# The slab behind a rewriting norm: its high part cut in quarters inside ScalarE's loop, its low part in halves between two evacuations, and TensorE begun by halves

## The chip, the cores and the metric

The kernel runs on one core of a Trainium2 chip. The metric is the device time of one launch in microseconds (us). Shown is the median of three runs; the profile is a fourth execution.

## The reference, cut to what matters

The model is a stack of four transformer-like layers on 512 tokens of width 1024: two of one kind and two of a second kind. In the second kind a layer begins with a norm that is modulated by a condition:

```python
shift1, scale1, gate1, shift2, scale2, gate2 = jnp.split(mod[:, None, :], 6, axis=-1)
h = rms_norm_2(x, norm1) * (1.0 + scale1) + shift1
proj = h @ w_in
```

The product `h @ w_in` has 1816 columns: a pooling part `u`, queries `q`, keys and values `kv` of three branches, and 24 gates. They feed a pooling mixer and sparse attention. After them come an output projection, a second norm and a feed-forward part. The change concerns only the first projections of these two layers, so it acts at two places of the run. They are called place 1 (layer 0 of the second kind, about 2015 to 2110 us of the profile) and place 2 (layer 1, about 2615 to 2710 us).

## The kernel before

**Slabs.** All weights pass through two slab buffers of 128 x 2048 words. SyncE loads slab i into `raw[i % 2]` with two DMAs of 512 KB (L323), once the low part of slab i-2 is made. ScalarE rounds it to `w_hi` (L329) and VectorE subtracts to get `w_lo` (L333). TensorE then forms `w_hi*h_hi + w_hi*h_lo + w_lo*h_hi` in three matmuls for each 128 x 128 block (`THREE`). A slab of a projection has 256 output columns: eight row blocks k of 256 words each, so words 0 to 1023 hold k = 0 to 3. It fills two PSUM banks, "piece" 0 and 1. One call of `proj_piece_T` makes 24 matmuls (L384) for one piece.

**The rewriting norm.** Call the slabs at such a norm S, S+1, S+2 and so on. TensorE multiplies slab S by `x` times the gain alone, before the norm's factor `rstd` is known; the norm's sums and its broadcast are formed between these matmuls. Once `rstd` is known the activations are rewritten with their factor and shift, for the slabs that follow. Per row block i, VectorE makes `nbuf` (L2460), ScalarE makes `h_hi` (L1942) and VectorE makes `h_lo` (L2467); TensorE's chunk i of slab S+1 (six matmuls, L459) waits for `h_lo` i. VectorE's step i+1 of L2460 comes before its step i of L2467. After its eight steps ScalarE goes on to `beside_projection`.

**What follows the loop.** For slab S the helper `beside_projection` has ScalarE make `w_hi` of slab S+2 (L329). VectorE takes the two banks of slab S out with the factor `rstd` (L1510, each adding 1 to the semaphore `scaled`). It then waits for both, adds to `evac_dve`, and makes `w_lo` of slab S+2 (L333). ScalarE adds a bias to the two results (L1520). TensorE starts slab S+2 once `w_lo_done`, `evac_act` and `evac_dve` are there.

**What waits for `scaled` besides.** SyncE's queue is one sequence: two loads of compression weights of 1 MB each with a small one behind each (L1317, L1319), then the load of slab S+2, then

```python
sp.wait_ge(s["scaled"], 2 * (ph[1] + 1))
sp.dma_start(pool_w, ...)                      # L1322
```

and only behind it the load of slab S+3. `pool_w` lies in the buffer `rstd`, which both evacuations read.

**From slab S+3 back to TensorE.** For slab S+1 ScalarE makes `w_hi` of slab S+3 first (it waits for the load), and then copies one bank out (L1525). VectorE waits for that copy, builds the compression windows (four operations at L2847) and then makes `w_lo` of slab S+3 (L333, a "late" split). TensorE, done with slab S+2, forms head sums (16 small matmuls, L959) and then begins slab S+3 in a helper that fills in between the compression matmuls (L604, L1858). Its first matmul needs `w_lo` of slab S+3.

Every place where a part of a slab is split is written out by hand; nothing plans it.

Of the kernel before, what the change touches and what calls it, by code (L numbers as in the profile page):

```python
# [58 lines left out]
class Cursor:  # L59


    def __init__(self):
        self.slab = 0
        self.proj = 0
        self.outp = 0
        self.outs = 0
        self.norm = 0
        self.sq = 0
        self.chain = 0
        self.roots = 0  # L70
        self.bcasts = 0
        self.hnorms = 0
        self.order = range(KC)
        self.fresh = False
        self.pending_split = None
        self.late_split = None
        self.pending = None
        self.swiglus = 0
        self.deferred = False
        self.rope = 0  # L80
        self.moved = 0
        self.hn = 0
        self.hnsq = 0
        self.hnb = 0
        self.ret = 0
        self.retg = 0
        self.att = 0
        self.attg = 0
        self.yt = 0
        self.sb = 0  # L90
        self.sbh = 0
        self.pool = 0
        self.base = 0
        self.mid = None
        self.soon = None
        self.third = None
        self.oq = 0
        self.begun = 0
        self.gates = 0
        self.mod = None  # L100
        self.rstds = 0
        self.added = 0
        self.kinds = 1
        self.rewrite = False
        self.first_scaled = False
        self.scaled = 0
        self.rewrites = 0
        self.final = None
        self.mods = 0
        self.just_out = False  # L110
        self.ffs = 0

# [15 lines left out]
def hybrid_stack_kernel(nc, A, out, stop=None):  # L128
# [87 lines left out]
    with ExitStack() as ctx:  # L216
# [78 lines left out]
        s = {}  # L295
        for name in [
            "in_loaded", "first_loaded", "first_hi", "first_lo", "zeroed", "consts_loaded", "bank_done", "bcast_done", "gate_normed", "norm_chain", "x_final", "w_hi_done",
            "w_lo_done", "slab_used", "evac_act", "evac_dve", "a_hi_done", "a_lo_done", "up_normed", "x_ready",
            "sq_done", "sq_added", "sums_done", "sums_copied", "ssq_done", "rms_done", "rstd_done", "h_full", "u_used", "gm_joined", "scaled", "pool_loaded", "h_hi_done", "h_lo_done", "rope_cos",
            "rope_rot", "rope_moved", "rope_sin", "rope_done", "hn_sq", "hn_sum", "hn_ms", "hn_rms", "hn_chain", "hn_bcast",  # L300
            "hn_done", "dv_half", "dv_first", "ff_scaled", "bias_col", "dec_loaded", "ret_s", "ret_p", "ret_o", "ret_copy", "ret_mean", "ret_cen", "ret_gate",
            "ret_y", "att_s", "att_max", "att_exp", "att_t", "att_pt", "att_o", "att_rec", "att_r", "att_rc", "att_w",
            "att_y", "sb_z", "sb_abs", "sb_e", "sb_ln", "sb_sp", "sb_msk", "sb_high", "sb_low", "sb_sum",
            "sb_cut", "sb_a", "sb_exp", "sb_o", "sb_y", "pl_sum", "pl_tail", "pl_x", "pl_mm", "gate_t",
            "gate_sig", "cm_w", "cm_kp", "cm_h", "cm_act", "cm_o", "cm_k", "kd_copy", "cb_s", "cb_sm",
            "cb_sub", "cb_exp", "cb_t", "cb_pt", "cb_mix", "cb_o", "cb_w", "cb_y", "nh_mm", "nh_t", "nh_v", "oq_hi", "oq_lo", "oq_mm", "oq_x", "om_hi", "om_lo", "om_mm", "om_x", "y6_hi", "y6_lo", "mod_silu", "mod_mul", "mod_add", "mod_red",
            "mod_row", "mod_col", "mod_bias", "gmod_one", "gmod_done", "stored", "dve_chain", "act_chain",
            "v_bd",
        ]:
            s[name] = sem(name)  # L310
# [35 lines left out]
        def part_lo(eng, i, part, parts):  # L346

            if part == 0:
                eng.wait_ge(s["w_hi_done"], i + 1)
            cols = slice(part * SLAB // parts, (part + 1) * SLAB // parts)  # L350
            ins = eng.tensor_tensor(w_lo[:, i % 2, cols], raw[:, i % 2, cols], w_hi[:, i % 2, cols].bitcast(F32), ALU.subtract)
            if part == parts - 1:
                ins.then_inc(s["w_lo_done"], 1)

        def step_range(c, n, last):

# [19 lines left out]

        THREE = ((0, 0), (0, 1), (1, 0))

        def proj_piece_T(pe, e, bank, piece, inc, soon=None):
            wbuf, hbuf = (w_hi, w_lo), (h_hi, h_lo)  # L380
            for k in range(KC):
                for n, (a, b) in enumerate(THREE):
                    at = k * 256 + piece * P
                    mm = pe.matmul(ps[:, bank], wbuf[a][:, e % 2, at:at + P], hbuf[b][:, k],  # L384
                                   start=(k == 0 and n == 0), stop=(k == KC - 1 and n == 2))
                if k == 2 and soon:
                    soon()
            if inc:
                mm.then_inc(s["slab_used"], 1)
# [55 lines left out]
        def pe_first_proj(pe, c):  # L445
# [70 lines left out]
            c.rewrite = False  # L516
            c.slab += 1
            c.proj += 1
            return 2

        def pe_proj(pe, c, n, kind):
# [10 lines left out]
            c.just_out = False  # L532
            s0, q0 = c.slab, c.proj

            def step(j, e):
                pe.wait_ge(s["w_lo_done"], j + (s0 + 1))
                if not isinstance(j, int) or q0 + j >= 2:
                    pe.wait_ge(s["evac_act"], j + (q0 - 1))
                    pe.wait_ge(s["evac_dve"], j + (q0 - 1))
                bank = 4 + 2 * ((q0 + e) % 2)  # L540
# [945 lines left out]
        def beside_projection(eng, c, ph, last, split, mine, name, next_ph=None, only=None):  # L1486
            for i in range(len(ph[2])) if only is None else [only]:
                eng.wait_ge(s["slab_used"], c.slab + 1)
                bank = 4 + 2 * (c.proj % 2)
                then_split = False  # L1490
                if split is None:
                    pass
                elif i < len(ph[2]) - 1 or next_ph not in LATE[mine]:
                    then_split = mine == 1 and (c.first_scaled or i == len(ph[2]) - 1 and next_ph == "stick")
                    if not then_split:
                        split(eng, c.slab + 2, c.slab)
                else:

                    c.late_split = lambda n=c.slab: split(eng, n + 2, n)
# [6 lines left out]
                elif c.first_scaled and mine == 1:  # L1506
                    eng.wait_ge(s["rstd_done"], c.rstds)
                    for piece in range(2):
                        dst, src = evac_projection(ph, i, bank, piece)
                        eng.tensor_tensor(dst, src, rstd[:, :], ALU.mult).then_inc(s["scaled"], 1)  # L1510
                    c.scaled += 2
                    eng.wait_ge(s["scaled"], c.scaled)
                    eng.sem_inc(s[name], 1)
                elif c.first_scaled:
                    l = c.rewrites - 1
                    eng.wait_ge(s["bias_col"], 16)
                    for piece in range(2):
                        dst, _ = evac_projection(ph, i, bank, piece)
                        eng.wait_ge(s["scaled"], c.scaled + piece + 1)
                        ins = eng.activation(dst, dst, ACT.Identity, bias=n_bias[:, 2 * l + piece:2 * l + piece + 1])  # L1520
# [5 lines left out]
                elif ph[0] in ("projT", "retention") and mine == 1:  # L1526

                    eng.wait_ge(s["rstd_done"], c.rstds)
                    for piece in range(2):
                        dst, src = evac_projection(ph, i, bank, piece)  # L1530
                        scale = ph[4] if ph[0] == "projT" and ph[4] is not None and i < 2 else 1.0
                        ins = eng.scalar_tensor_tensor(dst, src, scale, rstd[:, :], ALU.mult, ALU.mult)
# [353 lines left out]
        def _(eng):  # L1886
            act_e = nc.scalar
            c = Cursor()
# [5 lines left out]
            for pi, ph in enumerate(phases):  # L1894
                last = pi == last_slabs
                if ph[0] == "norm":
# [35 lines left out]
                    if not c.deferred:  # L1932
                        c.hnorms += 1
                        c.first_scaled = True
                        for i, k in enumerate(c.order):
# [3 lines left out]
                            else:  # L1939
                                eng.wait_ge(s["slab_used"], c.slab + 1)  # L1940
                            at = ph[2][0] * 48 + ph[2][1] * KC + k
                            eng.activation(h_hi[:, k], nbuf[:, i % 2], ACT.Identity, bias=mods[:, at:at + 1]  # L1942
                                           ).then_inc(s["h_hi_done"], 1)
                        c.mods += KC
                        c.rewrites += 1
                    c.bcasts += 1 if ph[3] is None else 2
# [1060 lines left out]
```

## Time and profile before

| what | us |
|---|---|
| median of three runs | 3227.76 |
| lowest, highest | 3224.59, 3228.41 |
| the profiled execution's own time | 3233.87 |
| its span, first to last instruction | 3232.1 |
| TensorE busy | 3201.2 (99%) |
| VectorE busy | 1689.2 (52%) |
| ScalarE busy | 1141.9 (35%) |
| mean granted TensorE clock | 0.996 |

In a timeline row the first number is the start in us from the span's start, the second the time taken. Then come engine, line, operation and operands. A bracket at the end gives how long the engine sat idle before it and what ended that. Matmuls overlap: a row of 0.39 us is followed by the next after 0.23 us, so starts are what to compare.

### The profile page before, as it was taken

The numbers are of one execution on the slowest core, as the hardware profiler recorded it, in microseconds if no ns is written. First come the engines' busy times: TensorE is split into PE (matmuls) and PEld (weight loads), VectorE is DVE, ScalarE is ACT, GpSimd is POOL, SyncE is SP. The second block draws the span as 40 slices with busy tenths as digits, with TensorE's granted clock in tenths as the row PEclk, the third lists the DMA queues.
The fourth block names the chain that finished last, engine by engine and source line by source line (L and its number), as shares of the span: only waits on it lengthen the run. The fifth ranks groups of instructions, "written<-read, shape, count | busy, mean of one in ns | idle before, by whom it ended". The sixth has DMA issues, their size and how long they took to land.

```text
span 3232.1 us, 40590 instructions
## 1 busy us (share of the span) xinstructions
PE 3201.2 (99%) x15504; PEld 2525.9 (78%) x15504; DVE 1689.2 (52%) x2139; ACT 1141.9 (35%) x1683; POOL 1281.9 (40%) x688
## 2 busy tenths in 40 slices
PE   9999999999999999999999999999999999999999
PEld 7888886788888888887678888765888878578887
DVE  4454456554445445446765444765655455665443
ACT  3222312532223222237652222456332343752222
POOL 4777101057772777400016774030577102017600
PEclk9999999999999999999999999999999998999999
DMA  6554331145443554321124543411444242024332
GB/s 208 152 150 156 121 113 59 53 145 155 143 153 113 145 152 154 127 94 41 51 79 138 150 148 110 97 60 40 143 143 152 96 97 86 27 89 152 125 97 85
DMA packets 338468, 371.48 MB, mean 115 GB/s; under 512 B 32560, under 2 KB 287664, under 8 KB 338224
## 3 DMA queue, kind: packets, MB, share of 16 engines
q1 hardware_dynamic: 310896, 277.99, 27.9%
q0 software_dynamic: 27456, 91.94, 9.2%
q8 instruction: 74, 1.21, 0.2%
q14 instruction: 42, 0.34, 0.0%
HBM read 361.92 MB, written 2.18 MB: 113 GB/s over the span
## 4 chain that ended last, share of the span: by engine, by line
PE 46%; DVE 2%; ACT 2%; issue 1%; ACTq 0%; DVEq 0%
PE ps L384 19%; PE ps L748 16%; PE ps L459 1%; PE ps L664 1%; PE ps L1041 1%; PE ps L1072 1%; PE ps L1084 1%; PE ps L604 1%; PE ps L564 1%; PE ps L1858 1%; PE ps L546 0%; PE ps L959 0%; DVE nbuf L2460 0%; ACT p_bufs L1099 0%; DVE h_lo L2467 0%
## 5 line engine op out<-in xcount | busy, mean ns | idle before, releaser
L329 ACT CAST w_hi<-raw 128x2048 fp32r<-128x2048 f32 x246 | 469.4, 1908 | 1132.6 <-PE ps L384 927.5
L384 PE MATMUL ps<-h_hi,w_hi 128*128 128x512 f32 x2064 | 808.2, 392 | 4.4 <-DVE w_lo L333 4.4
L384 PE MATMUL ps<-h_lo,w_hi 128*128 128x512 f32 x2064 | 805.0, 390 | 0.0
L384 PE MATMUL ps<-h_hi,w_lo 128*128 128x512 f32 x2064 | 804.8, 390 | 0.0
L333 DVE TENSOR_TENSOR w_lo<-raw,w_hi 128x2048 fp32r<-128x2048 f32 x244 | 623.9, 2557 | 255.9 <-ACT w_hi L329 255.1
L748 PE MATMUL ps<-a_hi,w_hi 128*128 128x512 f32 x1328 | 517.7, 390 | 1.9 <-DVE act L2510 1.4
L748 PE MATMUL ps<-a_hi,w_lo 128*128 128x512 f32 x1328 | 516.8, 389 | 0.0
L748 PE MATMUL ps<-a_lo,w_hi 128*128 128x512 f32 x1328 | 516.7, 389 | 0.0
L384 PEld LDWEIGHTS ps<-h_hi,w_hi 128*128 128x128 f32 x2064 | 388.5, 188 | 86.8 <-issue 6.6
L384 PEld LDWEIGHTS ps<-h_hi,w_lo 128*128 128x128 f32 x2064 | 388.5, 188 | 81.6
L384 PEld LDWEIGHTS ps<-h_lo,w_hi 128*128 128x128 f32 x2064 | 388.6, 188 | 79.9 <-issue 0.2
L2242 POOL TENSOR_TENSOR m_acc<-m_acc,m_in 128x1024 f32<-128x1024 f32 (+1 forms) x147 | 374.5, 2547 | 12.3
L860 DVE TENSOR_TENSOR a_lo<-act,a_hi 128x1024 fp32r<-128x1024 f32 x82 | 124.7, 1528 | 382.1 <-ACT a_hi L845 381.8
L748 PEld LDWEIGHTS ps<-a_hi,w_hi 128*128 128x128 f32 x1328 | 249.2, 188 | 58.9 <-issue 7.5
L748 PEld LDWEIGHTS ps<-a_lo,w_hi 128*128 128x128 f32 x1328 | 249.3, 188 | 51.8
L748 PEld LDWEIGHTS ps<-a_hi,w_lo 128*128 128x128 f32 x1328 | 249.2, 188 | 51.7
L2228 POOL TENSOR_SCALAR m_in<-m_in,c_act 128x1024 f32<-128x1024 f32 x84 | 283.5, 3375 | 4.5
L2493 DVE TENSOR_TENSOR stage<-ps,rstd 128x512 f32<-128x512 f32 x88 | 60.8, 691 | 400.3 <-PE ps L384 391.5
L845 ACT CAST a_hi<-act 128x1024 fp32r (+1 forms) x82 | 85.3, 1049 | 468.8 <-PE ps L748 468.8
L2228 POOL TENSOR_SCALAR m_in<-m_in,mods 128x1024 f32<-128x1024 f32 (+1 forms) x70 | 211.0, 3017 | 5.5 <-DMA m_in<-in_w_in 2.3
L2246 POOL PARTITION_ALL_REDUCE m_in<-m_acc x21 | 125.8, 5990 | 127.1 <-issue 127.1
L2222 POOL DMA_DIRECT2D m_in<-in_w_ff x64 | 38.8, 606 | 307.6 <-ACT rstd L1930 273.8
(365 smaller groups left out, 4017.6 us busy)
## 6 DMA issues: line engine op xcount, KB each, us to landing
raw<-in_ffn_w_in SPq DMA_DIRECT2D x174, 512.0 KB, 5.1
raw<-in_w_ff SPq DMA_DIRECT2D x128, 512.0 KB, 4.3
m_in<-in_w_mod POOLq DMA_DIRECT2D x96, 512.0 KB, 4.1
raw<-in_ffn_w_out SPq DMA_DIRECT2D x88, 512.0 KB, 4.2
m_in<-in_w_ff POOLq DMA_DIRECT2D x64, 512.0 KB, 4.1
raw<-in_hyb_w_in SPq DMA_DIRECT2D x28, 512.0 KB, 4.5
raw<-in_w_in SPq DMA_DIRECT2D x28, 512.0 KB, 4.7
raw<-in_sb_w_in SPq DMA_DIRECT2D x24, 512.0 KB, 4.2
```

What stands on the lines that cost most here:

```text
L329: eng.copy(w_hi[:, e % 2], raw[:, e % 2]).then_inc(s["w_hi_done"], 1)
L333: eng.tensor_tensor(w_lo[:, e % 2], raw[:, e % 2], w_hi[:, e % 2].bitcast(F32), ALU.subtract).then_inc(s["w_lo_done"], 1)
L384: mm = pe.matmul(ps[:, bank], wbuf[a][:, e % 2, at:at + P], hbuf[b][:, k], start=(k == 0 and n == 0), stop=(k == KC - 1 and n == 2))
L459: mm = pe.matmul(ps[:, bank + piece], wbuf[a][:, c.slab % 2, at:at + P], hbuf[b][:, k], start=(i == 0 and n == 0), stop=(i == KC - 1 and n ...
L748: mm = pe.matmul(ps[:, d], wbuf[a][:, (s0 + e) % 2, at:at + P], abuf[b][:, (r0 + e) % 2, half * SEQ:(half + 1) * SEQ], start=(first and m ...
L845: eng.copy(a_hi[:, (c.outp + e) % 2].rearrange("p (a t) -> p a t", a=2), src).then_inc(s["a_hi_done"], 1)
L860: eng.tensor_tensor(a_lo[:, r].rearrange("p (a t) -> p a t", a=2), src, a_hi[:, r].bitcast(F32).rearrange("p (a t) -> p a t", a=2), ALU.su ...
L2222: eng.dma_start(dst, src(k)).then_inc(loaded[k % 2], 16)
L2228: ins = eng.tensor_scalar(dst[:, cols], m_in[:, k % 2, cols], col(k, r), None, ALU.mult)
L2242: eng.tensor_tensor(acc, acc, rows_in, ALU.add).then_inc(s["mod_add"], 1)
L2246: eng.partition_all_reduce(m_in[:, 0, 0:width], m_acc[:, 0:width], P, RADD).then_inc(s["mod_red"], 1)
L2493: eng.tensor_tensor(st[:, 0:SEQ], ps[:, bank], rstd[:, :], ALU.mult).then_inc(s["gate_normed"], 1)
```

## The change

ScalarE's rewriting loop gets a quarter of the high part of slab S+2 after each of its steps 3 to 6. VectorE makes the first half of the low part after the first evacuation and the second half after the second one. A new semaphore `w_lo_half` marks the first half. TensorE's first piece of slab S+2 starts on that half and the first evacuation. After row block k = 3 it waits for the whole low part, and before the second piece for the second evacuation. The waits on `evac_act` and `evac_dve` before this slab go. The code of SyncE is not changed.

```diff
         def part_lo(eng, i, part, parts):
...
             ins = eng.tensor_tensor(w_lo[:, i % 2, cols], raw[:, i % 2, cols], w_hi[:, i % 2, cols].bitcast(F32), ALU.subtract)
             if part == parts - 1:
                 ins.then_inc(s["w_lo_done"], 1)
+            return ins
...
-        def proj_piece_T(pe, e, bank, piece, inc, soon=None):
+        def proj_piece_T(pe, e, bank, piece, inc, soon=None, soon_at=2):
...
-                if k == 2 and soon:
+                if k == soon_at and soon:
                     soon()
...
+            def first_by_piece():
+                bank = 4 + 2 * (q0 % 2)
+                pe.wait_ge(s["w_lo_half"], c.rewrites)
+                pe.wait_ge(s["scaled"], 2 * c.rewrites - 1)
+                proj_piece_T(pe, s0, bank, 0, False, lambda: pe.wait_ge(s["w_lo_done"], s0 + 1), 3)
+                pe.wait_ge(s["scaled"], 2 * c.rewrites)
+                proj_piece_T(pe, s0, bank + 1, 1, True)
+
             def step(j, e):
+                if c.by_piece:
+                    c.by_piece = False
+                    first_by_piece()
+                    return
                 pe.wait_ge(s["w_lo_done"], j + (s0 + 1))
...
-                if split is None:
+                if split is None or c.first_scaled:
                     pass
                 elif i < len(ph[2]) - 1 or next_ph not in LATE[mine]:
-                    then_split = mine == 1 and (c.first_scaled or i == len(ph[2]) - 1 and next_ph == "stick")
+                    then_split = mine == 1 and i == len(ph[2]) - 1 and next_ph == "stick"
...
                     for piece in range(2):
                         dst, src = evac_projection(ph, i, bank, piece)
                         eng.tensor_tensor(dst, src, rstd[:, :], ALU.mult).then_inc(s["scaled"], 1)
+                        low = part_lo(eng, c.slab + 2, piece, 2)
+                        if piece == 0:
+                            low.then_inc(s["w_lo_half"], 1)
                     c.scaled += 2
                     eng.wait_ge(s["scaled"], c.scaled)
                     eng.sem_inc(s[name], 1)
...
                             eng.activation(h_hi[:, k], nbuf[:, i % 2], ACT.Identity, bias=mods[:, at:at + 1]
                                            ).then_inc(s["h_hi_done"], 1)
+                            if 3 <= i < 7:
+                                part_hi(eng, c.slab + 2, i - 3, 4)
```

The helper `part_hi`, which the kernel had before, waits at part 0 for the slab's load and for slab i-2 to be used, and adds to `w_hi_done` after the last part:

```python
if part == 0:
    eng.wait_ge(w_loaded[i % 2], i * 16 + (32 - 16 * (i % 2)))
    eng.wait_ge(s["slab_used"], i - 1)
```

## Rows read from the trace of the kernel before

**Rows 1.** Waits of TensorE over the run: total us, times, longest.

```profile
PE ps L384 <- DVE w_lo L333: 4.4, 3, 1.6
```

**Rows 2.** Timeline of TensorE, place 1.

```profile
2055.35 0.39 PE L459 MATMUL ps<-h_hi,w_lo 128*128 128x512 f32 x1
2057.19 0.47 PE L384 MATMUL ps<-h_hi,w_hi 128*128 128x512 f32 x1 [1.45 <-DVE w_lo L333]
...
2068.19 1.84 PE L959 MATMUL ps<-consts,nbuf 128*128 128x2 f32 x16
2069.89 0.49 PE L604 MATMUL ps<-h_hi,w_hi 128*128 128x512 f32 x1
```

**Rows 3.** Timeline of TensorE, place 2.

```profile
2647.86 0.39 PE L459 MATMUL ps<-h_hi,w_hi 128*128 128x512 f32 x1
...
2654.81 0.47 PE L384 MATMUL ps<-h_hi,w_hi 128*128 128x512 f32 x1 [1.35 <-DVE w_lo L333]
...
2665.82 1.84 PE L959 MATMUL ps<-consts,nbuf 128*128 128x2 f32 x16
2667.81 0.47 PE L604 MATMUL ps<-h_hi,w_hi 128*128 128x512 f32 x1
```

**Rows 4.** Timeline of VectorE, place 1.

```profile
2053.36 1.28 DVE L1510 TENSOR_TENSOR act<-ps,rstd 128x512 f32<-128x512 f32 x2
2054.80 2.29 DVE L333 TENSOR_TENSOR w_lo<-raw,w_hi 128x2048 fp32r<-128x2048 f32 x1 [0.15 <-DVE act L1510]
...
2063.55 3.83 DVE L2847 TENSOR_TENSOR scr<-act,params 128x496 f32<-128x496 f32 x4 [0.60 <-ACT act L1525]
2067.29 2.29 DVE L333 TENSOR_TENSOR w_lo<-raw,w_hi 128x2048 fp32r<-128x2048 f32 x1
...
2071.98 1.23 DVE L980 TENSOR_TENSOR act<-hn_s 128x1024 f32<-128x1024 f32 x1
```

**Rows 5.** Timeline of SyncE's DMA queue, place 1.

```profile
2038.73 1.15 SPq L323 DMA_DIRECT2D raw<-in_w_in  x2
...
2054.67 0.37 SPq L1322 DMA_DIRECT2D rstd<-in_pool_w  x1
```

**Rows 6.** Place 1: landing after issue of slab S+2's two DMAs.

```profile
DMA to landing us min/median/max: 4.8/5.1/5.5
```

**Rows 7.** Timeline of ScalarE, place 1.

```profile
2046.13 0.73 ACT L1942 ACTIVATE h_hi<-nbuf,mods 128x512 fp32r<-128x512 f32 x1 [0.72 <-DVE nbuf L2460]
...
2061.13 1.91 ACT L329 CAST w_hi<-raw 128x2048 fp32r<-128x2048 f32 x1 [5.43 <-DMA raw<-in_w_in]
```

**Rows 8.** Lines by form: ScalarE on a quarter slab.

```profile
L342 ACT CAST w_hi<-raw 128x512 fp32r<-128x512 f32 x16 | 9.9, 619 | 0.0
```

**Rows 9.** Place 2: slab S+2's two DMA issues, and their landing after issue.

```profile
2640.86 1.15 SPq L323 DMA_DIRECT2D raw<-in_w_in  x2
...
DMA to landing us min/median/max: 5.0/5.4/5.7
```

**Rows 10.** Timeline of ScalarE, place 2: step 3 of the loop.

```profile
2643.76 0.72 ACT L1942 ACTIVATE h_hi<-nbuf,mods 128x512 fp32r<-128x512 f32 x1 [0.72 <-DVE nbuf L2460]
```

**Rows 11.** Timeline of VectorE, place 2: `h_lo` of step 4, `w_lo` of slab S+3.

```profile
2646.54 0.75 DVE L2467 SCALAR_TENSOR_TENSOR h_lo<-nbuf,mods,h_hi 128x512 fp32r<-128x512 f32 x1
...
2665.33 2.27 DVE L333 TENSOR_TENSOR w_lo<-raw,w_hi 128x2048 fp32r<-128x2048 f32 x1
```

**Rows 12.** Windows of TensorE: us, busy (matmuls), granted clock, DMA share, GB/s.

```profile
2702.00:2704.00 2.00, 2.00 (x7) 0.50 1.03 356
```

**Rows 13.** Timeline of TensorE: at full clock, a stretch of small matmuls, and a lower clock.

```profile
2071.47 1.12 PE L1858 MATMUL ps<-scr 64*64 64x31 f32 x32
...
2076.65 1.04 PE L987 MATMUL ps<-consts,act 128*128 128x128 f32 x8
...
2080.35 0.63 PE L604 MATMUL ps<-h_hi,w_hi 128*128 128x512 f32 x1
...
2083.05 1.52 PE L1858 MATMUL ps<-scr 64*64 64x31 f32 x32
```

More of the change, by code:

```diff
@@ L109, in __init__ @@
         self.mods = 0
+        self.by_piece = False
         self.just_out = False
@@ L298, in hybrid_stack_kernel @@
             "w_lo_done", "slab_used", "evac_act", "evac_dve", "a_hi_done", "a_lo_done", "up_normed", "x_ready",
-            "sq_done", "sq_added", "sums_done", "sums_copied", "ssq_done", "rms_done", "rstd_done", "h_full", "u_used", "gm_joined", "scaled", "pool_loaded", "h_hi_done", "h_lo_done", "rope_cos",
+            "sq_done", "sq_added", "sums_done", "sums_copied", "ssq_done", "rms_done", "rstd_done", "h_full", "u_used", "w_lo_half", "gm_joined", "scaled", "pool_loaded", "h_hi_done", "h_lo_done", "rope_cos",
             "rope_rot", "rope_moved", "rope_sin", "rope_done", "hn_sq", "hn_sum", "hn_ms", "hn_rms", "hn_chain", "hn_bcast",
@@ L518, in pe_first_proj @@
             c.proj += 1
+            c.rewrites += 1
+            c.by_piece = True
             return 2
```

## The prediction

> **What bounds the kernel now.** I began with the page's busy times: TensorE is busy 99% of the span, in the table above. So whatever moves the end must move a start on TensorE. The waits of TensorE come next: it waits for `w_lo` three times, 4.4 us in all [rows 1]. The timelines of TensorE show that two of the three are the waits at which the change aims. In place 1 the last matmul of slab S+1 starts at 2055.35, the next could start 0.23 later, at 2055.58, and slab S+2 starts at 2057.19, so 1.61 us are lost [rows 2]. In place 2 chunk 4 of slab S+1 starts at 2647.86; four chunks of six matmuls at 0.227 us end at 2653.30; slab S+2 starts at 2654.81, so 1.51 us are lost [rows 3].
>
> The question is then what binds the next start, that of slab S+3 (L604). Its `w_lo` ends at 2665.33 + 2.27 = 2667.60 in place 2 and TensorE starts at 2667.81, 0.21 later, where the 16 sums in front of it would have let it start 1.70 after 2665.82, at 2667.52 (the distance in place 1) [rows 2, 3, 11]. In place 1 `w_lo` ends at 2067.29 + 2.29 = 2069.58, and with the same 0.21 it allows 2069.79 against the 2069.89 seen: 0.10 of slack [rows 2, 4]. So slab S+3 arrives just in time at both places, though the trace books no wait there at place 1. A slab S+2 that ends earlier gains at most 0.10 us unless slab S+3 comes earlier too.
>
> Where `w_lo` of slab S+3 comes from I followed backwards: VectorE starts it right behind the windows of L2847, which waited for ScalarE's copy; ScalarE made `w_hi` first, at 2061.13, after 5.43 us of idling for the load [rows 4, 7]; SyncE issues that load behind `pool_w`, at 2054.67, and that waits for `scaled`, which VectorE completes at 2053.36 + 1.28 = 2054.64 [rows 4, 5]. That is a chain in which each link idles for the one before. Its start is the **second evacuation**, which the change moves.
>
> **The change part by part.**
>
> *VectorE's order.* Before: two evacuations, a wait, one subtraction of 2.29 us [rows 4]. Each evacuation lets the next begin after 0.60 (1.28 for two less 0.68 for one). Half a subtraction has 1024 columns; the nearest row, a subtraction's kind of operation on 1024 columns, takes 1.23 us, and the next can begin about 0.09 earlier, at 1.13 (0.09 is also the overlap in 2.29 against a next start 2.20 later) [rows 4]. Bounds: 1.05, half of 2.20 less its own start, and 1.30. So the second evacuation begins 1.13 later and `scaled` is complete **1.13 us later** (1.05 to 1.30). The whole sequence ends at 2053.36 + 0.60 + 1.13 + 0.60 + 1.22 = 2056.91, against 2057.09: the 0.15 idle for its own evacuation goes, and one start is added. On VectorE alone the change costs nothing.
> The Trainium skill ("VectorE: DVE Perf Modes", section on the TRN2 errata) states a fixed cost per instruction that halving pays twice, (N+151)/0.96 ns for this operation; that gives 2.29 us whole, as the trace has it, and 1.22 a half. By it the shift would be 1.13 too and the sum the same.
>
> *TensorE's start by halves.* At place 1 slab S+2 may start once the first half is there, at 2053.36 + 0.60 + 1.22 = 2055.18, before TensorE is ready at 2055.58. Four row blocks take 12 matmuls, 2.72 us, to 2058.30; the second half is there at 2056.91. So the wait of 1.61 us goes. Slab S+2 ends near 2066.6 instead of 2068.19, and nothing takes up the time.
>
> *SyncE, not edited but late.* `pool_w` and slab S+3's load move by 1.13 at place 1, and with them `w_hi`, the copy, the windows and `w_lo`, each of which has idle time ahead of it or stands directly behind one that has [rows 4, 5, 7]. `w_lo` ends at 2070.71, L604 starts at 2070.92 instead of 2069.89: **+1.03 us at place 1**, the gain included. If a transfer stream that starts later lands no later, it is 0 to -0.10; if all shifts by 1.30, it is +1.20.
>
> *ScalarE's quarters.* A quarter takes 0.62 us [rows 8] and the idle time between two steps of the loop is 0.72 [rows 7]. ScalarE and VectorE take turns with a period of 1.45, and the quarter's own 0.52 (0.62 less the same overlap) fits. But part 0 waits for slab S+2's load, and behind it in ScalarE's queue stands `h_hi` of step 4, for which VectorE's `h_lo` and TensorE's chunk 4 wait. At place 1 the second DMA, issued about 0.59 after 2038.73, lands 5.5 later, at 2044.8 [rows 5, 6]; part 0 comes at 2046.13 + 0.63 = 2046.76, so nothing waits. At **place 2** the same DMA is issued at about 2641.45 and lands 5.7 later, at **2647.15** [rows 9], and part 0 comes at 2643.76 + 0.63 = 2644.39 [rows 10]: ScalarE stands for 2.8 us. Then part 0 goes from 2647.20, `h_hi` 4 from 2647.72 to 2648.44, `h_lo` 4 from 2648.50 instead of 2646.54, **1.96 later** [rows 11]. The pair keeps its period, so the end of the loop and the first evacuation are 1.96 later too. TensorE starts chunk 4 at 2649.35 instead of 2647.86 [rows 3], then is held to VectorE's period, and ends slab S+1 at 2655.06 (four chunks of 1.36, 0.09 for each restart) instead of 2653.30. The first half of `w_lo` is there at 2654.8, so slab S+2 starts at 2655.06, 0.25 later than before: all that the start by halves gained at place 2 goes here.
>
> *Place 2, the chain.* `scaled` is complete 1.96 + 1.13 = 3.09 later, L604 starts at 2670.90: **+3.09 us**. Bounds: -0.2, if the load had landed in time and the chain shifted nothing, and +3.7, if the load lands 0.4 later and halves take 1.30.
>
> *TensorE's clock.* From the end of slab S+2 to L604 TensorE now has only the 16 sums and then nothing: 2066.6 to 2070.92, 4.3 us, at place 1, and 2666.07 to 2670.90, 4.8 us, at place 2. Before, these stretches were 1.70 and 1.99 us and the clock stayed full. Elsewhere 3.70 us of small matmuls (2076.65 to 2080.35) were followed by a fall from 2.4 to 1.2 GHz [rows 13]. A fall costs: six matmuls in 2.70 us (2080.35 to 2083.05) in place of 1.58 (2069.89 to 2071.47), and 0.40 on the next group (1.52 against 1.12): 1.5 us [rows 2, 13]. One fall was longer: at 2702 the clock is at half for a full window of 2 us, with 7 matmuls where some 9 would go [rows 12]; I allow 3.1 us for such a one. Bounds for both places together: 0 and 6.2. I take three chances in four at each place, 2 x 0.75 x 1.5 = **2.3 us**.
> The Trainium skill ("TensorE: Matmul & The Clock Gate", "Why this matters for your kernels") says that an idle stretch long enough puts the array back to half clock. It speaks against this change; by that rule alone both places fall, and the term would be 3.0.
>
> *Sum.* 1.03 + 3.09 + 2.3 = **+6.4 us**. Against the profiled execution: 3233.87 + 6.4 = 3240.3, span 3238.5. That execution was 6.1 us above the median of the three runs, and all terms are differences within 200 us of it, so I carry them over: 3227.76 + 6.4 = **3234.2**. Nothing behind L604 gives it back: from there to 2110 and to 2710 TensorE books no wait, so it runs at its own pace.
>
> **The rivals.**
> 1. *The stall just goes.* TensorE starts slab S+2 early and the rest follows: -1.61 - 1.51 = -3.1, 3224.7. For it: the trace books no wait ahead of L604 at place 1, and place 2 is near it. Against it: L604 stands 0.21 behind `w_lo` in place 2 and the load of slab S+3 stands behind `scaled` in the queue. It decides if L604 has over 2.7 us of slack at place 1; I read 0.10. Chance 0.06.
> 2. *The load of place 2 is in time.* If slab S+2 lands by 2644.4, place 2 costs 1.13, as it has no slack: 1.03 + 1.13, and 1.5 of clock, is +3.7, 3231.5. For it: one landing of 5.7 was seen once. Against it: it would have to be 2.8 us shorter, and place 1 shows 5.5. Chance 0.12.
> 3. *The late loop costs more.* At place 2 the stop in chunk 4 brings the clock down in slab S+1 as well, or falls are long ones: +10, 3237.8. For it: the long fall at 2702. Against it: a stop of 1.5 us is shorter than the 1.99 after which the clock stayed full. Chance 0.10.
> The forecast, both chains late with some fall of the clock, has 0.72; its own range is 3230 to 3238.
>
> **How the numbers follow.** About 0.2% (6.5 us) can be told from no change. The forecast, at +6.4, lies on that bound: half of its 0.72 counts as slower, half as the same, 0.01 as faster by scatter. Rival 3 is slower, rival 2 nearly all the same, rival 1 mostly the same with 0.02 faster. Together 0.47 slower, 0.49 the same, 0.04 faster. The range leaves rival 1 and the dearest end of rival 3 out: 3229.0 to 3238.5.
>
> **What would show it.** Right: no wait before slab S+2 at place 1; `pool_w` issued 1.1 us later behind the evacuations; `w_hi` of slab S+3 at about 2062.3 and L604 at 2070.9; at place 2 ScalarE idle near 2.8 us before its first quarter, TensorE stopped at chunk 4, L604 at 2670.9; waits of L604 for `w_lo` of 2 to 3 us each, and a clock below full right behind them. Wrong: if L604 follows the sums without a wait at either place, or if no quarter waits for a load, the step concerned fails.

## The result, and the profile after

| | before | changed |
|---|---|---|
| median, us (seven runs each) | 3227.33 | 3239.34 |
| lowest, highest | 3224.50, 3228.41 | 3234.56, 3241.92 |
| the profiled execution's own time | 3233.87 | 3240.86 |
| its span | 3232.1 | 3239.1 |
| mean granted TensorE clock of it | 0.996 | 0.994 |

The ratio is 1.0032, with a 95% interval of 1.0023 to 1.0041: the changed kernel is slower by 12 us, 0.37% by the medians. The forecast was 3234.2 and its range ended at 3238.5, 0.8 us below the measured median. So the sign was right, and the size was too small by half, +6.4 against +12. The two profiled executions differ by only 7.0 us. That the medians differ by five more is the main thing to explain.

Line numbers of the changed kernel are a little higher: L386, L461, L620, L975 for TensorE's L384, L459, L604, L959; L334 and L330 for the splits L333 and L329; L343 and L352 are a quarter of the high part and a half of the low part.

**Place 1.** VectorE's timeline after the change, which answers to [rows 4]:

```profile
2052.48 0.69 DVE L1526 TENSOR_TENSOR act<-ps,rstd 128x512 f32<-128x512 f32 x1
2053.08 1.22 DVE L352 TENSOR_TENSOR w_lo<-raw,w_hi 128x1024 fp32r<-128x1024 f32 x1
2054.21 0.69 DVE L1526 TENSOR_TENSOR act<-ps,rstd 128x512 f32<-128x512 f32 x1
2054.81 1.22 DVE L352 TENSOR_TENSOR w_lo<-raw,w_hi 128x1024 fp32r<-128x1024 f32 x1
...
2063.78 3.81 DVE L2868 TENSOR_TENSOR scr<-act,params 128x496 f32<-128x496 f32 x4 [1.88 <-ACT act L1544]
2067.52 2.27 DVE L334 TENSOR_TENSOR w_lo<-raw,w_hi 128x2048 fp32r<-128x2048 f32 x1
```

A half takes 1.22 us and the second evacuation starts 1.13 after it, as forecast. TensorE, answering to [rows 2]:

```profile
2054.73 0.39 PE L386 MATMUL ps<-h_hi,w_hi 128*128 128x512 f32 x1
...
2065.61 1.84 PE L975 MATMUL ps<-consts,nbuf 128*128 128x2 f32 x16
2070.00 0.47 PE L620 MATMUL ps<-h_hi,w_hi 128*128 128x512 f32 x1 [2.54 <-issue]
```

Slab S+2 follows slab S+1 without a bracket. The same idle time now stands before slab S+3: 2.54 us, booked as "issue" though the start is 0.21 behind the end of `w_lo` (2067.52 + 2.27 = 2069.79). To compare the two traces I count from step 3 of the rewriting loop on ScalarE, at 2046.13 before [rows 7] and here at:

```profile
2045.25 0.73 ACT L1961 ACTIVATE h_hi<-nbuf,mods 128x512 fp32r<-128x512 f32 x1 [0.73 <-DVE nbuf L2481]
```

Slab S+3 starts 2069.89 - 2046.13 = 23.76 us after it before and 2070.00 - 2045.25 = 24.75 after it now: **0.99 us later**.

**Place 2.** ScalarE, answering to [rows 10], with step 3 and the first quarter:

```profile
2643.76 0.73 ACT L1961 ACTIVATE h_hi<-nbuf,mods 128x512 fp32r<-128x512 f32 x1 [0.72 <-DVE nbuf L2481]
2647.13 0.62 ACT L343 CAST w_hi<-raw 128x512 fp32r<-128x512 f32 x1 [2.65 <-DMA raw<-in_w_in]
2647.66 0.72 ACT L1961 ACTIVATE h_hi<-nbuf,mods 128x512 fp32r<-128x512 f32 x1
```

The quarter idles 2.65 us for the load and step 4 stands behind it. SyncE's queue, answering to [rows 9]:

```profile
2641.67 1.15 SPq L324 DMA_DIRECT2D raw<-in_w_in  x2
2655.30 0.37 SPq L1338 DMA_DIRECT2D rstd<-in_pool_w  x1
```

The two DMAs at 2641.67 load slab S+2, and they land this long after their issue:

```profile
DMA to landing us min/median/max: 4.0/4.4/4.8
```

TensorE, answering to [rows 3]:

```profile
2649.22 0.50 PE L461 MATMUL ps<-h_hi,w_hi 128*128 128x512 f32 x1 [1.20 <-DVE h_lo L2488]
...
2655.01 0.39 PE L386 MATMUL ps<-h_hi,w_hi 128*128 128x512 f32 x1
...
2665.89 1.84 PE L975 MATMUL ps<-consts,nbuf 128*128 128x2 f32 x16
2670.29 0.47 PE L620 MATMUL ps<-h_hi,w_hi 128*128 128x512 f32 x1 [2.56 <-issue]
```

Step 3 stands at 2643.76 in both traces, so slab S+3 is 2670.29 - 2667.81 = **2.48 us later**. The chain costs 0.99 + 2.48 = 3.47 us in all.

**The clock.** TensorE in windows of 2 us of the changed kernel; columns are the window, its length, busy time (matmuls), granted clock, DMA share, GB/s:

```profile
2068.00:2070.00 2.00, 0.00 (x1) 1.00 0.00 0
2070.00:2072.00 2.00, 2.00 (x6) 0.60 0.51 128
2072.00:2074.00 2.00, 2.00 (x34) 0.55 1.06 373
...
2670.00:2672.00 2.00, 1.71 (x6) 0.78 0.36 69
2672.00:2674.00 2.00, 2.00 (x32) 0.50 1.08 375
...
2686.00:2688.00 2.00, 2.00 (x32) 0.50 0.16 37
```

In this trace the clock is full up to the moment when slab S+3 starts and falls to half (1.2 of 2.4 GHz) within it, at both places. I added up, over all such windows, the time at half clock, (1 - clock) / 0.5 of each: 37.6 us in the changed kernel's trace and 28.5 in the one of before. Of the 28.5, 1.2 us lie behind TensorE's last matmul, so 27.3 can have cost anything. Both traces have falls near 1570 and 2104. What differs is this. At place 1 the fall of 3.4 us at 2070 stands for one of 3.4 at 2080. Place 2 has four falls of 6.8 us from 2670 on (at 2670, 2684, 2708 and 2738) where before had one of 3.4 and two of 6.8.

The 10.2 us more at half clock can cost TensorE at most half of that, 5.1 us. The traces bear this out: from step 3 of place 2, at 2643.76 in both, to the end of the span are 588.3 us before and 595.3 after, 7.0 more, and 2.48 of them are the chain. The other 4.5 us come behind slab S+3, where the clock falls. From step 3 of place 1 to step 3 of place 2 the changed kernel takes 0.88 us more. Ahead of place 1, where both kernels do the same, its execution happened to be 0.88 us shorter, so the two executions differ by 7.0 in all.

### The profile page after: what moved, and what is told of

It is laid out like the page before. It is cut to its first block and busy times, and to the rows that moved or that the text cites. A ratio compares the mean times of both kernels' runs of the same rounds, so it can differ in the third digit from the quotient of the medians.

```text
span 3239.1 us, 40596 instructions
## 1 busy us (share of the span) xinstructions
PE 3206.2 (99%) x15504; PEld 2529.5 (78%) x15504; DVE 1681.5 (52%) x2141; ACT 1143.5 (35%) x1689; POOL 1298.9 (40%) x688
## 5 line engine op out<-in xcount | busy, mean ns | idle before, releaser
L330 ACT CAST w_hi<-raw 128x2048 fp32r<-128x2048 f32 x244 | 465.9, 1909 | 1127.4 <-PE ps L386 922.0
L386 PE MATMUL ps<-h_hi,w_hi 128*128 128x512 f32 x2064 | 808.0, 391 | 1.6 <-DVE w_lo L334 1.6
L386 PE MATMUL ps<-h_lo,w_hi 128*128 128x512 f32 x2064 | 804.8, 390 | 0.0
L386 PE MATMUL ps<-h_hi,w_lo 128*128 128x512 f32 x2064 | 804.7, 390 | 0.0
L334 DVE TENSOR_TENSOR w_lo<-raw,w_hi 128x2048 fp32r<-128x2048 f32 x242 | 601.2, 2484 | 254.0 <-ACT w_hi L330 253.8
L386 PEld LDWEIGHTS ps<-h_hi,w_hi 128*128 128x128 f32 x2064 | 388.5, 188 | 83.1 <-issue 3.0
L386 PEld LDWEIGHTS ps<-h_hi,w_lo 128*128 128x128 f32 x2064 | 388.6, 188 | 81.1
L386 PEld LDWEIGHTS ps<-h_lo,w_hi 128*128 128x128 f32 x2064 | 388.6, 188 | 80.4 <-issue 0.2
L2263 POOL TENSOR_TENSOR m_acc<-m_acc,m_in 128x1024 f32<-128x1024 f32 (+1 forms) x147 | 386.7, 2631 | 12.3
```

Of the source, the lines that this page charges most:

```text
L330: eng.copy(w_hi[:, e % 2], raw[:, e % 2]).then_inc(s["w_hi_done"], 1)
L334: eng.tensor_tensor(w_lo[:, e % 2], raw[:, e % 2], w_hi[:, e % 2].bitcast(F32), ALU.subtract).then_inc(s["w_lo_done"], 1)
L2263: eng.tensor_tensor(acc, acc, rows_in, ALU.add).then_inc(s["mod_add"], 1)
```

## The experiments

**The theory** after this result: the change costs some 3.5 us because slab S+3 comes later (VectorE's order at both places, the load at place 2), and the rest because TensorE now idles 2.5 us behind 1.84 us of small sums and its clock falls more often. **The rivals:** the quarters and halves cost engine time that reaches the path, so that each part costs by itself; or the clock differs by chance, and filling the idle time changes nothing.

Since the clock differs from run to run, each run's time was set against its mean granted clock. One slope for all kernels, with a constant for each, fits the 199 runs with a scatter of 1.26 us left over: **2.84 us (2.67 to 3.01) for each 0.001 of mean clock**. That is near what it must be: 0.001 of the mean is 3230 x 0.001 / 0.5 = 6.5 us at half clock, and a TensorE that is always busy loses half of it, 3.2. The clock of a run is on record to 0.001 only, which flattens a fitted slope. By an estimate from the scatter of the clock within a kernel, 0.00104, and the rounding error, 0.00029, it is 8% too flat. With 3.1 in its place the changed kernel would be 2.7 to 2.9 us above before at the same clock, not 3.2 to 3.6. "Same clock" below is the time that the fit gives at a clock of 0.998. The last column does not come from the fit: it is the distance from step 3 of the loop to the first matmul of slab S+3 in each kernel's trace, place 1 and place 2, less that of before (23.76 and 24.05). Each is read from one execution. The twelve traces check the price of the clock as well: a trace's span less the sum of its last column grows by 0.48 us for each us at half clock ahead of TensorE's last matmul, and no trace is off that line by more than 1.6 us.

| kernel | median us (runs) | ratio, 95% interval | mean clock | same clock | traces |
|---|---|---|---|---|---|
| before, with the first four | 3227.64 (35) | | 0.9971 | 3226.2 ±0.4 | |
| before, with the second four | 3228.29 (33) | | 0.9973 | 3226.1 ±0.5 | |
| before, with the last two | 3228.59 (17) | | 0.9969 | 3226.1 ±0.6 | |
| changed, first | 3239.34 (7) | 1.0032, 1.0023 to 1.0041 | 0.9947 | 3229.4 ±1.1 | +0.99, +2.48 |
| e9 changed again | 3239.02 (6) | 1.0036, 1.0022 to 1.0050 | 0.9945 | 3229.7 ±1.2 | +0.87, +1.92 |
| e1 load ahead | 3230.67 (12) | 1.0007, 0.9997 to 1.0016 | 0.9965 | 3226.3 ±0.8 | -0.77, -0.59 |
| e2 evacuations first | 3233.72 (11) | 1.0012, 1.0003 to 1.0022 | 0.9962 | 3228.2 ±0.8 | -0.10, +0.80 |
| e3 kept busy | 3232.55 (11) | 1.0013, 1.0004 to 1.0021 | 0.9973 | 3231.2 ±0.8 | +1.12, +4.23 |
| e4 load ahead alone | 3227.51 (11) | 0.9996, 0.9988 to 1.0005 | 0.9974 | 3226.1 ±0.8 | 0.00, -0.33 |
| e5 quarters late | 3235.18 (11) | 1.0023, 1.0013 to 1.0032 | 0.9956 | 3228.5 ±0.9 | +1.29, +0.98 |
| e6 order alone | 3233.97 (11) | 1.0015, 1.0006 to 1.0024 | 0.9965 | 3229.3 ±0.8 | +1.60, +1.27 |
| e7 both | 3224.49 (11) | 0.9992, 0.9983 to 1.0001 | 0.9973 | 3223.2 ±0.8 | -0.78, -1.93 |
| e8 before kept busy | 3232.46 (11) | 1.0014, 1.0005 to 1.0023 | 0.9975 | 3231.0 ±0.8 | +2.41, +2.12 |
| e10 both again | 3226.87 (12) | 0.9991, 0.9983 to 1.0000 | 0.9971 | 3224.1 ±0.7 | -0.79, -1.93 |

**e1_load_ahead.** The changed kernel, with slab S+3's load issued ahead of the wait for `scaled` and of `pool_w` in SyncE's queue.

```diff
-                elif ph[0] == "nsa_pre" and ph[2] == 1:
+                elif ph[0] == "nsa_pre" and ph[2] == 2:
```

> The changed kernel, with one edit on SyncE's queue: slab S+3's load is issued ahead of the wait for scaled and of pool_w, no longer behind them. Theory A (the late second evacuation holds back slab S+3's load, and TensorE's idling for it brings its clock down): the 5 us of idling ahead of slab S+3 go at both places, that slab starts 1.7 to 2 us after the head sums do, the two falls of the clock right behind it go, and the time is 3224 to 3227, at or below the kernel before. Rival B (the quarters in ScalarE's loop and the stop at place 2 cost the time): the stop at place 2 is still there, and the time stays above 3234. Rival C (most of the 12 us is scatter of the clock that has nothing to do with the idling): 3232 to 3236, the 3.5 us of the chain less.

At place 1 the load has landed when ScalarE comes to it (no bracket), and TensorE waits 0.82 us instead of 2.54; at place 2 not at all:

```profile
2054.67 1.89 ACT L330 CAST w_hi<-raw 128x2048 fp32r<-128x2048 f32 x1
...
2067.35 0.47 PE L620 MATMUL ps<-h_hi,w_hi 128*128 128x512 f32 x1 [0.82 <-issue]
...
2667.61 0.49 PE L620 MATMUL ps<-h_hi,w_hi 128*128 128x512 f32 x1
```

Of the 12 us 8.7 go: 3239.3 to 3230.7, at the same clock from +3.2 against before to +0.1, and the clock rises from 0.9947 to 0.9965. So the wait for `scaled` in SyncE's queue is the link through which VectorE's order hurts. The time is still above the range of theory A, 3224 to 3227. The clock stays below that of before: the trace has no fall right behind slab S+3 at either place, but two of 6.8 us further on, near 2099 and 2130. The traces say 1.36 us less than before; the fit shows none of it (+0.1, give or take 0.9). Some 1 us is unexplained here.

**e2_evacuations_first.** The changed kernel, with both evacuations ahead of both halves.

```diff
                         eng.tensor_tensor(dst, src, rstd[:, :], ALU.mult).then_inc(s["scaled"], 1)
+                    for piece in range(2):
                         low = part_lo(eng, c.slab + 2, piece, 2)
```

> The changed kernel, with both evacuations ahead of the two halves of the low part. scaled is then complete as early as before the change, and TensorE starts slab S+2 0.2 us later than it could. Theory A: place 1's slab S+3 is back at its old time (within 0.2 us), place 2's is about 1.4 to 2 us late, from the stop in ScalarE's loop alone; but TensorE still idles ahead of it (1.3 to 1.6 us at place 1, more at place 2), so some falls of the clock stay: 3229 to 3235. Rival B: no better than the changed kernel, 3238 to 3240.

The waits for slab S+3 shrink from 2.5 to about 1 us, and slab S+3 starts 1.09 sooner than in the changed kernel at place 1 (the 1.13 of the order) and 1.68 sooner at place 2, where the load was also 0.6 us less late. The time lies in the range of theory A, and place 1 is back at its old time as it said; place 2 is only 0.80 late, where it said 1.4 to 2. The same-clock time falls by 1.2 us (1.5 against e9), where the first trace of the changed kernel says 2.8 and e9's says 2.1. That leaves about 1 us open, little more than the intervals. The clock stays below that of before: at place 2 it fell right behind a wait of 1.02 us.

```profile
2069.23 0.47 PE L620 MATMUL ps<-h_hi,w_hi 128*128 128x512 f32 x1 [1.09 <-issue]
...
2671.02 0.47 PE L620 MATMUL ps<-h_hi,w_hi 128*128 128x512 f32 x1 [1.02 <-issue]
```

**e3_kept_busy.** The changed kernel, with ten matmuls of 512 columns, whose result nobody reads, between the sums and slab S+3 at both places.

```diff
+                        keep_warm(pe, 2, 10)
                         fill = dense_T(pe, c, 1)
```

> The changed kernel, with ten matmuls of no use (2.3 us, to a bank that is free) between the head sums and slab S+3, where TensorE idled 2.5 us. Theory A: the chain is as late as in the changed kernel, 1.0 and 2.5 us, but the clock does not fall at slab S+3; the time is 3230 to 3233, and what it is below 3239.3 is the price of the clock. Rival C: the falls are as many as before, 3238 to 3240. If the falls only move on to the next small matmuls: 3234 to 3238.

```profile
2066.19 1.84 PE L975 MATMUL ps<-consts,nbuf 128*128 128x2 f32 x16
2068.32 2.56 PE L398 MATMUL ps<-h_hi 128*128 128x512 f32 x10 [0.28 <-DVE scr L2869]
2070.71 0.39 PE L620 MATMUL ps<-h_hi,w_hi 128*128 128x512 f32 x1
```

The windows that were at 0.60, 0.55, 0.50 and 0.50 after the change are full here:

```profile
2070.00:2072.00 2.00, 2.00 (x10) 1.00 0.23 32
2072.00:2074.00 2.00, 2.00 (x37) 1.00 0.99 333
2672.00:2674.00 2.00, 2.00 (x37) 1.00 1.09 384
2686.00:2688.00 2.00, 2.00 (x32) 1.00 0.04 8
```

The mean clock over eleven runs is 0.9973, that of before. The kernel does more, has a same-clock time 1.8 us longer than the change, and is still 6.8 us faster by the medians, as theory A said. That shows the clock term by itself: (0.9973 - 0.9947) x 2.84 / 0.001 = 7.4 us. Its trace says 1.9 us longer too, but at place 2 slab S+1 took 7.21 us from chunk 4 on in place of 5.79, so 1.4 of the 1.9 us are the price of a fall of the clock and not of the chain. In this trace the clock fell once inside slab S+1 of place 2, 1.4 us behind the end of the stop for `h_lo`, where the row of a matmul grows from 0.39 to 0.63 us, which is the mechanism of my third rival:

```profile
2648.88 0.50 PE L461 MATMUL ps<-h_hi,w_hi 128*128 128x512 f32 x1 [1.81 <-DVE h_lo L2489]
...
2650.92 0.63 PE L461 MATMUL ps<-h_lo,w_hi 128*128 128x512 f32 x1
```

**e8_before_kept_busy.** The control: the same ten matmuls in the kernel before.

```diff
+                        keep_warm(pe, 2, 10)
                         fill = dense_T(pe, c, 1)
```

> The kernel before, with the same ten matmuls of no use ahead of slab S+3 at both places: a control for the third experiment. Nothing hides them here, so at equal clock +4.2 to +4.6. If they only fill an idle stretch in the changed kernel, the mean granted clock here stays that of the kernel before (0.9971 to 0.9975), and the time is 3231.5 to 3233. If such matmuls by themselves keep the clock up later too, the mean clock rises above 0.998 and the time is 3229 to 3231.

```profile
2068.72 2.57 PE L396 MATMUL ps<-h_hi 128*128 128x512 f32 x10
...
2668.71 2.57 PE L396 MATMUL ps<-h_hi 128*128 128x512 f32 x10
```

The first row is place 1, the second place 2. The ten matmuls cost 4.9 us at the same clock (4.5 by the traces), and the clock is 0.9975 against 0.9973, both as forecast. The filler as such raises nothing that can be told from the scatter: it helps where TensorE would idle.

**e4_load_ahead_alone.** The kernel before, with only e1's edit.

```diff
-                elif ph[0] == "nsa_pre" and ph[2] == 1:
+                elif ph[0] == "nsa_pre" and ph[2] == 2:
```

> The kernel before, with slab S+3's load ahead of the wait for scaled, and nothing else. Theory A with my reading that slab S+3 was just in time: slab S+3 starts 0.1 us earlier at place 1 and 0.3 at place 2, 3226 to 3227.5. If slab S+3's load were the larger limit: over 1.5 us less. If an earlier load does harm (by colliding with slab S+2's load or the compression weights): over 3229.

No difference that can be measured, at the same clock 3226.1 against 3226.2, and slab S+3 starts 0.0 and 0.33 us earlier (forecast 0.1 and 0.3). So e1's gain is not a saving that the kernel before had lying about: there slab S+2 itself ends late, and slab S+3 ahead of it buys nothing.

**e6_order_alone.** The kernel before, with only VectorE's order: a half of the low part behind each evacuation, no early quarters and no start by halves. TensorE waits for `evac_dve` as before.

```diff
                         eng.tensor_tensor(dst, src, rstd[:, :], ALU.mult).then_inc(s["scaled"], 1)
+                        part_lo(eng, c.slab + 2, piece, 2)
...
-                if then_split:
+                if then_split and not c.first_scaled:
```

> The kernel before, with only VectorE's order changed: first evacuation, first half of the low part, second evacuation, second half. ScalarE's whole high part stays behind the loop, TensorE's waits are the old ones. The first half has to wait for w_hi, so scaled is complete about 1.7 us later. Theory A: slab S+3's load and its low part are 1.5 to 1.7 us late at both places, with no stop in the loop and no start by halves: +3.0 to +3.4 at equal clock, plus 1 to 5 us of clock, 3231 to 3236. If the place in VectorE's order did not matter: TensorE's start of slab S+2 alone is 0.3 us late, 3228.

```profile
2053.59 1.22 DVE L351 TENSOR_TENSOR w_lo<-raw,w_hi 128x1024 fp32r<-128x1024 f32 x1 [0.45 <-ACT w_hi L329]
...
2070.59 0.47 PE L604 MATMUL ps<-h_hi,w_hi 128*128 128x512 f32 x1 [1.12 <-issue]
```

Here the half also waits 0.45 us for ScalarE's whole `w_hi`, and `scaled` with it: 1.13 + 0.45 is, to 0.02, the 1.60 by which slab S+3 is later at place 1. At place 2 it is 1.27 later, less than the 1.5 to 1.7 of the forecast. The same-clock time is 3.2 us longer, by the traces 2.9. So VectorE's order alone, with no quarters in ScalarE's loop and no start by halves, makes slab S+3 late at both places.

**e5_quarters_late.** The changed kernel, with the quarters behind steps 5, 6, 7 and the end of the loop, so that the load of place 2 has two periods more to land.

```diff
-                            if 3 <= i < 7:
-                                part_hi(eng, c.slab + 2, i - 3, 4)
+                            if i >= 5:
+                                part_hi(eng, c.slab + 2, i - 5, 4)
+                        part_hi(eng, c.slab + 2, 3, 4)
```

> The changed kernel, with ScalarE's quarters at steps 5, 6 and 7 of the loop and the fourth behind it, so that slab S+2 has landed at place 2 (2647.1) when the first quarter comes (2647.3). Theory A: no stop in chunk 4 at place 2; slab S+3 is still late there by the order of VectorE alone, 1.0 to 1.1 us in place of 2.5; place 1 as in the changed kernel, +1.0. At equal granted clock that is +2.1 against the kernel before (the changed kernel: +3.2 to +3.5), and TensorE still idles ahead of slab S+3, so falls of the clock stay: 3232 to 3237 in all. Rival B (the stop is the main cost): 3227 to 3230.

```profile
2654.33 0.62 ACT L343 CAST w_hi<-raw 128x512 fp32r<-128x512 f32 x1 [0.86 <-DMA raw<-in_w_in]
...
2674.88 0.47 PE L620 MATMUL ps<-h_hi,w_hi 128*128 128x512 f32 x1 [2.70 <-issue]
```

ScalarE's stop shrinks from 2.65 to 0.86 us. It does not go, as the forecast said, because slab S+2 lands 4.48 us after step 3 of the loop here, where it was 3.37 in the first trace of the changed kernel. Slab S+3 is 1.50 us less late at place 2 and 0.30 us later at place 1, and the same-clock time is 0.9 to 1.2 us shorter. The idle time ahead of slab S+3 stays at 2.7 to 2.9 us, and the clock stays low, 0.9956 against the 0.9973 of before. So most of the loss of clock comes without most of the stop. A share of the stop in it isn't excluded: the clock rises by 0.0009 from the changed kernel to e5, and by 0.0006 to 0.0008 from e1 to e7 and e10 below, which differ from e1 by the place of the quarters alone. Each step has an interval about as wide as itself, and e3, which has the stop, reaches the clock of before.

**e7_both** and **e10_both_again.** The edits of e1 and e5 together, on the changed kernel, run on two occasions. **e9_changed_again** is the changed kernel with no edit, beside e10.

```diff
-                elif ph[0] == "nsa_pre" and ph[2] == 1:
+                elif ph[0] == "nsa_pre" and ph[2] == 2:
...
-                            if 3 <= i < 7:
-                                part_hi(eng, c.slab + 2, i - 3, 4)
+                            if i >= 5:
+                                part_hi(eng, c.slab + 2, i - 5, 4)
+                        part_hi(eng, c.slab + 2, 3, 4)
```

> The changed kernel, with slab S+3's load ahead of the wait for scaled and the quarters late. Theory A: no stop at place 2, no idling for the load at either. Place 1 gains 0.8 us against the kernel before (VectorE's windows then limit it, as the trace of the first experiment shows), place 2 gains 1.5 to 1.7: -2.3 to -2.5 at equal clock, 3223.5 to 3226, the best so far. If the start by halves is worth nothing at place 2 either: 3226 to 3228.

> The changed kernel itself, unedited, timed beside the best one on the same chip, because its 12 us rest on seven runs. Theory A (3.5 us of lateness ahead of slab S+3 and the rest granted clock): at equal clock +3.2 to +3.6 against the kernel before, mean granted clock 0.0020 to 0.0028 below the kernel before's, median 8 to 12 us above it. If the first seven runs were chance: a median less than 6 us above.

> The kernel with slab S+3's load ahead and the quarters late, again, since its interval reached to no change. Theory A: -2.3 to -3 at equal clock, the clock of the kernel before, median 2 to 4 us below it.

```profile
2065.98 1.84 PE L975 MATMUL ps<-consts,nbuf 128*128 128x2 f32 x16
2068.64 0.47 PE L620 MATMUL ps<-h_hi,w_hi 128*128 128x512 f32 x1 [0.82 <-issue]
...
2662.77 1.84 PE L975 MATMUL ps<-consts,nbuf 128*128 128x2 f32 x16
2664.47 0.49 PE L620 MATMUL ps<-h_hi,w_hi 128*128 128x512 f32 x1
```

Slab S+3 starts 0.8 and 1.9 us earlier than before, in both runs of the kernel. The medians are 3224.49 and 3226.87, the lowest of the table, and the same-clock times lie 2.9 and 2.0 us below those of before. The first is in its forecast range; the second, 1.7 us below before, is just short of the 2 to 4 forecast. Both intervals of the ratio reach to 1, 0.9992 (0.9983 to 1.0001) and 0.9991 (0.9983 to 1.0000), so it is a gain of about 0.1% that either measurement barely shows.

The change repeated, e9, is as slow as at first, 1.0036, so its 12 us were not chance. Its trace has TensorE at place 2 like this:

```profile
2664.46 1.84 PE L975 MATMUL ps<-consts,nbuf 128*128 128x2 f32 x16
2668.86 0.76 PE L620 MATMUL ps<-h_hi,w_hi 128*128 128x512 f32 x1 [2.56 <-issue]
...
2666.00:2668.00 2.00, 0.30 (x3) 0.67 0.00 0
```

The window is one of those with the clock. Here the clock falls while TensorE waits, before slab S+3 starts at 2668.86, and stays at half for 10.2 us. In e6's trace it falls in the wait of place 2 too.

## Why the prediction was right in its chain and wrong in its size

- **TensorE's start by halves.** Right: slab S+2 follows without a wait at place 1, and at place 2 it starts at 2655.01 (forecast 2655.06).
- **VectorE's order.** Right: the second evacuation 1.13 later, and +0.99 at place 1 (forecast 1.03). e2 and e6 show the same price from two sides.
- **SyncE, not edited but late.** Right: `pool_w` and the load behind it carry the delay on, and e1 takes it away by moving one load ahead.
- **ScalarE's quarters at place 2.** Right in what happens: a quarter waits for the load, ScalarE idled 2.65 (forecast 2.8), TensorE stopped at chunk 4, and e5 confirms the cause. That the load landed at 2647.1, against a forecast of 2647.15, is luck: its second DMA was issued 0.8 us later than before and landed 4.8 us after issue in place of 5.7, and the two cancel. In e9 the same stop was 2.13 us.
- **Place 2, the chain.** A little too dear: `pool_w` was issued at 2655.30 instead of 2652.29, 3.01 later (forecast 3.09), but ScalarE's `w_hi` of slab S+3 began at 2661.65 instead of 2659.15, only 2.50 later. The load's second DMA took 5.3 us from issue to landing where it had taken 5.8. So +2.48 and not +3.09, and the chain is 3.47 and not 4.12. The same-clock times say +3.2 and +3.6; the second trace of the changed kernel, e9's, says +2.79, with the shorter stop of ScalarE.
- **TensorE's clock.** This is the term that failed. It was put at 2.3 us, with bounds of 0 and 6.2, and measured some 7: 6.9 in e9's means and 7.4 by e3. The price of one fall was about right (up to 1.7 us for one of 3.4 us and 3.4 for one of 6.8; I had 1.5 and 3.1). The chance of a first fall, three in four at each place, was not the fault: it came at both places in both traces of the changed kernel. The length and the count were wrong. I counted one short fall at each place; in the first trace the fall at place 2 is long and three more long ones follow, each in or behind a stretch of small matmuls that the kernel before has too. In e9's trace there are two at place 2, of 10.2 and 6.8 us. In the means of e9, 3239.67 against 3229.10, 10.6 us: 3.6 at the same clock and (0.99694 - 0.99450) x 2.84 / 0.001 = 6.9 of clock. At 6.5 us for 0.001 that is 16 us more at half clock, some five falls of 3.4 or two and a half of 6.8.
- **Against which time the sum was made.** The profiled execution of before was 6 us above the median, and I carried its differences over. Its trace has 28.5 us at half clock, where the mean of a run, 0.9972, is 0.0028 x 6.5 / 0.001 = 18. So the trace that I read had falls already near 2080, 2678, 2702 and 2732, in the very region, and they are enough for its excess. That the changed kernel has such falls in most runs is a reading of its mean clock; two executions of it were traced, and both have them. The surcharge of the clock on that trace is smaller than on the median: 4.5 us against some 7. I had the number (6.1 above the median) and the windows, and didn't put them together.
- **The rivals.** The first (the stall just goes) and the second (load in time) fell with the traces. The third had the right size, +10, by luck: its fall within slab S+1 was seen in one trace, e3's, and in neither of the changed kernel, and e5 without most of the stop is still low in clock. Long falls it did foresee. In the changed kernel they come ahead of slab S+3, in the wait, or within it, and further on.

The Trainium skill ("TensorE: Matmul & The Clock Gate", section "What's actually happening") takes the ramp penalty for under 1% of a typical span, and advises against fitting a model to its exact length. It speaks of the stretch at the lower clock with which matmuls begin. The falls in mid-run here are under 1% too, 7 of 3239 us is 0.2%, but that is about 60% of what the change does. Where the prediction uses the Trainium skill's page "TensorE: Matmul & The Clock Gate" ("Why this matters for your kernels"), it counts the 16 sums as part of the idle stretch, while the page speaks of idle gaps between bursts of matmuls. The gaps themselves were 2.54 and 2.56 us, and half clock followed at both places, as the prediction had it.

Not settled: why further falls follow the first one at place 2, what share the stop in ScalarE's loop has in the clock, and the 1.4 us between traces and fit in e1 and e2. In the other nine kernels they agree within 0.8, in e3 only if the fall in slab S+1 is counted in.

## What to carry to other kernels

When a wait is removed, look for where the next operand of the same engine comes from; one that arrives just in time shows no wait in the trace, and a queue that is not edited (here a small load that waits in SyncE's program order) can carry the delay on to it. Idle time that is moved is not the same idle time: behind a stretch of small matmuls it can bring the clock down, and that can cost more than the wait. If the profiled execution is well above the median, find out first what it has more of, and estimate the change against both.

## What the hardware showed that was not expected

- The scatter between runs is nearly all TensorE's clock: 2.84 us for each 0.001 of mean clock, with 1.26 us left.
- A wait of 1.45 us between full groups of matmuls [rows 2] left the clock full, while one of 2.54 us behind the 1.84 us of the 16 small sums was followed by half clock at both places, as it was in e9 (2.46 and 2.56 us) and in e6 (1.12 and 1.06 us). In e2 1.02 us behind the same sums were followed by half clock at place 2 and 1.09 us at place 1 were not, and 0.82 us were at place 1 in e7, but not in e1. Ten matmuls without use in the gap kept the clock full there.
- Most falls in these traces last about 3.4 or 6.8 us; e9's has one of 10.2 and e6's one of 13.7.
- Place 2's load of 512 KB for slab S+3 that was issued 3 us later took 5.3 us to land in place of 5.8, and the one for slab S+2 that was issued 0.8 us later took 4.8 in place of 5.7. Why is not shown.
